# Expert weights scattered with an add instead of summed on VectorE, in an attention and expert block on one core

## The reference

```python
q = (xc @ wq).reshape(PEER_CHUNK, PEER_HEADS, 2, PEER_HALF)      # 8 heads, two halves of 128
s = jnp.einsum('thpd,hpnd->thpn', q, keys)                       # 128 keys for each half
s_top, i_top = lax.top_k(s, PEER_TOPK)                           # 16 of each
cand_s = s_top[:, :, 0, :, None] + s_top[:, :, 1, None, :]       # 16 x 16 pairs
cand_i = i_top[:, :, 0, :, None] * PEER_N_KEYS + i_top[:, :, 1, None, :]
best_s, best_pos = lax.top_k(cand_s, PEER_TOPK)                  # 16 experts of 16384
eid = jnp.take_along_axis(cand_i, best_pos, axis=-1)
w = jax.nn.softmax(best_s, axis=-1)
act = gelu(einsum('thkd,td->thk', u_tab[eid], xc))
y = einsum('thk,thkd->td', w * act, v_tab[eid])
```

## Time and profile before

| | |
|---|---|
| three runs, median | 2646.3 us (2643.31 to 2647.86) |
| the profiled execution | 2645.3 us |
| its span, first to last instruction | 2643.5 us |
| mean granted clock of TensorE | 0.982 |
| busy: TensorE / VectorE / ScalarE / GpSimd | 2525.4 / 1700.5 / 968.7 / 733.1 us |
| scatters (L2084) | 384, 403.9 us busy |

### The profile page before, as it was taken

How to read it: one execution, slowest core, us unless ns; L and a number is a source line. 1 busy time by engine, 2 the same in 40 slices (tenths; PEclk the granted TensorE clock), 3 DMA queues, 4 the chain that set the end, 5 groups by cost and what they waited for, 6 DMA issues and landing times.

```text
span 2643.5 us, 34998 instructions
## 1 busy us (share of the span) xinstructions
PE 2525.4 (96%) x11864; PEld 2101.3 (79%) x11864; DVE 1700.5 (64%) x3123; ACT 968.7 (37%) x1328; POOL 733.1 (28%) x646
## 2 busy tenths in 40 slices
PE   7998999898999999899999999999999988999998
PEld 3876878676888777778888899999998746788786
DVE  4787769676788888832222488878787594444434
ACT  3323853522233333334444333333334264222222
POOL 0000000000055556555556366666650000000000
PEclk9999999999999999999999999999999989999999
DMA  5221913254234444344454699999994201222221
GB/s 230 95 80 67 362 33 132 91 189 166 77 121 140 140 131 144 124 138 143 143 187 155 219 349 344 355 340 354 338 351 166 72 1 56 80 96 99 91 96 64
DMA packets 177218, 433.55 MB, mean 164 GB/s; under 512 B 32752, under 2 KB 81904, under 8 KB 176752
## 3 DMA queue, kind: packets, MB, share of 16 engines
q1 hardware_dynamic: 123888, 331.61, 36.7%
q0 software_dynamic: 34816, 67.41, 7.2%
q10 hardware_dynamic: 18432, 33.56, 3.4%
HBM read 371.48 MB, written 61.01 MB: 164 GB/s over the span
## 4 chain that ended last, share of the span: by engine, by line
PE 79%; DVE 14%; ACT 2%; issue 2%; DMA 2%; SPq 0%; POOL 0%; ACTq 0%; DVEq 0%
PE ps L460 16%; PE ps L462 15%; PE ps L461 15%; PE ps L759 8%; PE ps L760 8%; PE ps L761 8%; DVE wlo L1296 2%; PE ps L670 2%; PE ps L486 1%; PE ps L654 1%; DMA ar<-mod 1%; DVE ar L1340 1%; DVE ar L1939 1%; PE ps L505 1%; DVE ar L1793 1%
## 5 line engine op out<-in xcount | busy, mean ns | idle before, releaser
L1296 DVE TENSOR_TENSOR wlo<-raw,whi 128x1024 fp32r<-128x1024 f32 x426 | 521.0, 1223 | 624.2 <-ACT whi L882 622.6
L882 ACT ACTIVATE whi<-raw 128x1024 fp32r<-128x1024 f32 x426 | 451.0, 1059 | 683.2 <-PE ps L761 406.1
L2084 POOL DMA_INDIRECT w_scratch<-ar x384 | 403.9, 1052 | 1042.2 <-issue 818.5
L460 PE MATMUL ps<-b_hi,whi 128*128 128x512 f32 x1344 | 534.9, 398 | 28.8 <-DVE wlo L1296 19.8
L462 PE MATMUL ps<-b_hi,wlo 128*128 128x512 f32 x1344 | 526.0, 391 | 0.0
L461 PE MATMUL ps<-b_lo,whi 128*128 128x512 f32 x1344 | 525.8, 391 | 0.0
L759 PE MATMUL ps<-a_hi,whi 128*128 128x384 f32 x1024 | 345.7, 338 | 12.9 <-DVE a_lo L1844 12.9
L460 PE MATMUL ps<-a_hi,whi 128*128 128x512 f32 x832 | 336.5, 404 | 13.3 <-DVE wlo L1296 7.1
L760 PE MATMUL ps<-a_lo,whi 128*128 128x384 f32 x1024 | 344.6, 337 | 0.0
L761 PE MATMUL ps<-a_hi,wlo 128*128 128x384 f32 x1024 | 344.3, 336 | 0.0
L460 PEld LDWEIGHTS ps<-b_hi,whi 128*128 128x128 f32 x1344 | 253.9, 189 | 97.3 <-DVE wlo L1296 31.9
(11 more groups left out here) (249 smaller groups left out, 3072.4 us busy)
## 6 DMA issues: line engine op xcount, KB each, us to landing
raw<-panels SPq DMA_DIRECT2D x430, 512.0 KB, 3.4
gelu_scratch<-ar ACTq DMA_DIRECT2D x128, 256.0 KB, 2.1
w_scratch<-rstd SPq DMA_DIRECT2D x32, 768.0 KB, 11.0
ar<-w_scratch SPq DMA_DIRECT2D x128, 192.0 KB, 4.4
ar<-gelu_scratch SPq DMA_DIRECT2D x128, 192.0 KB, 5.3
ar<-mod SPq DMA_DIRECT2D x32, 512.0 KB, 5.4
ar<-panels SPq DMA_DIRECT2D x3, 2048.0 KB, 20.6
w_scratch<-ar POOLq DMA_INDIRECT x384
```

Source lines behind the costliest of these rows:

```text
L460: pe.matmul(bank, w_h, hi[:, k, :], start=(k == 0), stop=False)
L882: act.activation(whi[:, u % SPLIT, :], raw[:, u % RAW, :], ACT.Copy).then_inc(hi_ready, 1)
L1296: dve.tensor_tensor(wlo[:, u % SPLIT, :], raw[:, u % RAW, :], f32(whi[:, u % SPLIT, :]), ALU.subtract).then_inc(lo_ready, 1)
L2084: nc.gpsimd.indirect_dma_start(experts, bass.IndirectOffsetOnAxis(offs[:, k:k + 1], 0), vals[:, k:k + 1], None)\
```

## The change

The scatter gets `compute_op=ALU.add`, so that each element is added to what stands in the zeroed table. The sums over earlier heads are dropped: every head now writes its own weights with one copy, as the first head did. The low parts between the sums go with them, so that each head has eight from one end of `pair_tops` to the next, and `TOPS_AT` is given accordingly.

```diff
--- before.py
+++ after.py
@@ -67,7 +67,7 @@
 DN = GU + 2 * FT
 PANELS = DN + FT
 
-TOPS_AT = (13, 21, 30, 39, 49, 59, 70, 81)
+TOPS_AT = tuple(range(13, 77, 8))
 RAW = RAW_SLOTS
 SPLIT = 2
 BANKS = 4
@@ -1780,24 +1780,8 @@
                 a_ = slice(h * HK + DT * TOPK, (h + 1) * HK)
                 pick(dve.tensor_scalar(vals[:, a_].bitcast(U32), eid[:, a_], float(EV * P), None, ALU.add))
                 pick(dve.tensor_copy(w_pick[:, h * TOPK:(h + 1) * TOPK], w[:, DT, :]))
-                if h == 0:
-                    dve.tensor_copy(vals[:, 0:DT * TOPK], flat(w[:, 0:DT, :])).then_inc(pick_ready, DT)
-                    return
-                same = area(A_TK, TOPK, h, TOPK)
-                earlier = lambda ap, t: ap.rearrange("p (h t k) -> p h t k", t=TT, k=TOPK)[:, 0:h, t, :]
-                for t in range(DT):
-                    a_ = slice(h * HK + t * TOPK, h * HK + (t + 1) * TOPK)
-                    pick(dve.tensor_tensor(same, eid[:, a_].unsqueeze(2).unsqueeze(3).to_broadcast([P, TOPK, h, TOPK]),
-                                           earlier(eid, t).unsqueeze(1).to_broadcast([P, TOPK, h, TOPK]), ALU.is_equal))
-                    picked()
-                    pick(dve.tensor_tensor(same, same, earlier(flat(best), t).unsqueeze(1).to_broadcast([P, TOPK, h, TOPK]), ALU.mult))
-                    picked()
-                    pick(dve.tensor_reduce(more, same.rearrange("p a h k -> p a (h k)"), AX.X, ALU.add))
-                    picked()
-                    dve.tensor_tensor(vals[:, a_], w[:, t, :], more, ALU.add).then_inc(pick_ready, 1)
-                    dve.wait_ge(pick_ready, h * DT + t + 1)
-                    if t == 1 or h >= 3 and t == 2 or h >= 5:
-                        next_lo()
+                at_ = slice(h * HK, h * HK + DT * TOPK)
+                dve.tensor_copy(vals[:, at_], flat(w[:, 0:DT, :])).then_inc(pick_ready, DT)
 
             next_lo()
             fold_half(7, 0)
@@ -2081,7 +2065,7 @@
                         c = (h * DT + t) * TOPK + k % TOPK
                         if c % PACE == 0:
                             pool.wait_ge(lo_ready, WQ - U + PACE_AT + c // PACE)
-                        nc.gpsimd.indirect_dma_start(experts, bass.IndirectOffsetOnAxis(offs[:, k:k + 1], 0), vals[:, k:k + 1], None)\
+                        nc.gpsimd.indirect_dma_start(experts, bass.IndirectOffsetOnAxis(offs[:, k:k + 1], 0), vals[:, k:k + 1], None, compute_op=ALU.add)\
                           .then_inc(scattered[t], 16)
 
             for done in ge_out:
```

## The result

The changed kernel takes 2693.1 us (median of 4 runs, 2692.3 to 2694.9), the kernel before 2646.0 (4 runs): ratio 1.0179, 95% interval 1.0167 to 1.0191. The change makes it 47 us slower, where 2627.7 us was forecast. It is rival A.

A forecast was written before the change was run, and what follows sets the result against it. TensorE was taken as the bound (79% of the chain), stalled by VectorE's sums; -20.5 + 1.1 + 0.5 + 0.3 = -18.6 us from 2645.3 gave 2626.7, stated as 2627.7 given the runs' median 2646.3; range 2622 to 2650.

The forecast's parts named there:

- rival A: GpSimd's scatters break the pace: above 1.54 us each, every further 0.1 us costs 38 us; up to 2772 us; chance 0.15.
- step 5: GpSimd's adding scatters: at most the gather's 1.42 us each, 1.72 with the gap, hidden behind the 1.81 us pace.
- Steps 1 and 2: VectorE in the heads' stage: the sums' 20.5 us of TensorE stalls go; six late low parts of 0.76 us stay.
- Step 3: Behind the last head, a new TensorE stall before the token picks: 0.8 us idle, 1.1 us lost with the restart.
- Step 4: ScalarE's written-out panels end at 68 instead of 80, so three more loop rounds run, costing 0.5 us.
- the DMA side: Software queue: 0.02 us of each engine per scatter, 0.2 us if all eight elements travel singly, within 1.81 us.
- Step 6: Last scatter's landing at the stage's end: up to 1.5 us later is free; 0.3 us charged, bounds 0 and 3.1.
- Rival B: Another gap between low parts replaces the sums' stalls in each head: gain only 3.6 us, 2643 us; chance 0.04.
- rival C: Late landings, the scatter queue lagging a little: 5 to 15 us at the stage's end, 2633 to 2643 us; chance 0.07.

The follow-up runs named there:

- `plain_no_sums`: The changed kernel with the plain overwriting scatter instead of the adding one: 2645.7 us against 2666.1 for the kernel before, ratio 0.9932.
- `add_only`: The kernel before with only the add put on its scatter, sums and extra low parts kept: 2712.4 us against 2666.1, ratio 1.0180.
- `half_elements`: The changed kernel with each scatter on 64 partitions instead of 128: 2639.8 us, ratio 0.9973 to the kernel before.
- experiment 4: Scatters on 64 partitions instead of 128, in the changed kernel (`half_elements`, ratio 0.9973) and in `plain_no_sums` (2649.0 us against 2665.4).
- `add_from_3`: Against the kernel before: heads 0 to 2 keep sums and overwriting scatters, later heads add, scatter pace 6 per panel: 2622.2 us against 2646.3, ratio 0.9909.

## Why the prediction was wrong

The step that failed is step 5, the price of an adding scatter: "I take the value of the gather or less, which hides wholly behind the pace". The gather's 1.42 us was taken for the nearest row because it handles single elements; it is a plain copy all the same. The measured price is 1.54 us at the least and 1.68 on average. It lies between my bounds (0.96 and 1.92), and the point from which it decides, 1.54 us, was worked out under rival A. A second term was put at nothing: the eight row gathers that GpSimd issues among the scatters, 11.3 us, which bring that point down to 1.51 us, below even the shortest adding scatter. With both, rival A gives the rest: 384 scatters at the measured pitch of 2.01 us end near 1510, 65 us beyond 1441.7 plus the 2.8 us by which this trace runs late; a landing 0.4 us longer and a stage 1.5 us shorter than summed make the 67. For a term with so near a threshold, 0.58 us above the known duration and 0.12 above the value taken, 0.15 was too small a chance. That mean and median of a row differ should have entered too: the plain scatter has a mean of 1.05 and a median of 0.96, and it is the mean, plus the gap, that fills a pace.

The rest, point by point:

- Steps 1 and 2, the sums' stalls go and six head boundaries stay: right. (Step 2 speaks of three to four extra low parts of the sums; by TOPS_AT it was one to three a head. Nothing was worked out from it.) In the changed trace panels 21, 29, 37, 45, 53 and 61 begin late by 0.80 us each (6.24 instead of 5.44 between gelus), all others of the stage not at all until the last head.
- Step 3, the new stall behind the last head, 0.8 us idle and 1.1 lost: right. The gelus of panels 67 to 69 lie 6.81 and 5.20 us apart, 1.13 over two panels, and TensorE's row reads as forecast:

```profile
1044.57 0.50 PE L460 MATMUL ps<-b_hi,whi 128*128 128x512 f32 x1 [0.83 <-DVE wlo L1296]
```

- Step 4, 0.5 us for three more rounds of ScalarE's loop: wrong in sign. A round of four panels took 21.85 us in the changed kernel and 21.94 before, against 21.76 without a loss; 19 rounds lose 1.7 us, 16 rounds lost 2.9, so 1.2 us are won. That is why the stage gave 20.4 us where the sum of its terms had 18.9. The add isn't the reason: a round takes 21.85 us in `plain_no_sums` and 21.94 in `add_only` too. What in the edit on VectorE shortens it stays open.
- Step 5, the DMA side: the software queue's share over 780 to 1040 us rose from 1.3% to 19.5%, with 130 scatters:

```profile
q0 software_dynamic: 18576, 0.07, 19.5%
```

  That is 0.39 us of each engine per scatter, where 0.2 was my estimate for eight single transfers and 0.02 the row before; 144 packets a scatter (from the page: 43008 packets more, over 384 scatters, beside 32) fit that each of the 128 elements travels by itself, and so do the 80 of `half_elements` (18432 more over 384, beside 32). 0.39 us is far under the pace, so I take it that the engines weren't the limit, and panels still landed in time.
- Step 6, the tail: the landing took 1.7 us instead of 1.3, inside the free 1.5 us of slip. My 0.3 us for it wasn't needed.
- The sentence of the Trainium skill (DMA: Bandwidth & Descriptors, section SWDGE vs HWDGE vs iDMA) pointed at GpSimd's work as the place of the cost, and that was the place. The traces don't show descriptors being written, and by experiment 4 less than a quarter of the surcharge goes with the elements. What the fixed 0.45 us consists of stays open.
- Rival B (stalls stay) and rival C (a queue that lags a little) didn't happen.

## What to carry to other kernels

Before work is moved to an engine that is held back by a pace, write down how much room that pace leaves for one instruction, and take a price that no trace shows from the operation itself in a run of a few instructions; a row of another kind of operation isn't a bound when the room is a few tenths of a microsecond and the count is in the hundreds. And add up everything that the engine issues on the way, not only the instruction that was changed. An engine that is idle a third of the time (GpSimd before: 223.7 of 725 us) has no slack once the next stage waits for its last instruction: what counts is when that one can end, and starting earlier or mixing cheap and dear forms (plain scatters for the first heads, adding ones behind) is worth as much as a faster instruction. Two streams that meet at one point don't add their costs, so a gain on the one shows only after the other has been brought within it.

## What the runs showed of the hardware that was not expected

- An indirect scatter of 128 single elements takes GpSimd 0.96 us plain and 1.54 us with an add (medians); 64 elements take 0.90 and 1.41. If the time grows evenly between the two sizes, the add's surcharge is 0.45 us fixed and 1.0 ns an element.
- A scatter without an add makes 32 packets, with 128 elements as with 64. One with an add makes 144 and 80, and for 128 elements the time on each DMA engine goes from 0.02 to 0.39 us.
- The adding scatter's mean isn't one number, while its median stays at 1.54 or 1.55. The line's busy time and count in four stretches of the changed kernel (us, POOL busy, granted clock, DMA share, GB/s):

```profile
740.00:860.00 120.00, 102.01 (x60) 1.00 0.60 134
860.00:1040.00 180.00, 152.55 (x91) 1.00 0.64 144
1200.00:1440.00 240.00, 193.64 (x115) 1.00 0.65 158
1460.00:1505.00 45.00, 37.68 (x25) 0.50 0.23 0
```

  By busy time over count it is 1.70 and 1.68 us while VectorE works on the heads, 1.68 in the stretch with low parts only, and the timeline's rows read 1.54 to 1.56 when every other engine stands (the fourth stretch cuts scatters at its edges). Nor does the stage alone set it: 48 scatters in a row take 90.8 us in `add_from_3` (1213.96 to 1304.71) and 94.8 us in the same stretch of the changed kernel (1215.91 to 1310.70), gaps included. In every head the mean lies above the median because a few scatters take 2 to 3.5 us. What makes those few long wasn't tried. In the last of the four stretches the granted clock is 0.50, the lower of the two levels, while TensorE does nothing.
